# Mixers' last projections cut into pieces with their layer norm following, and the last expert's selection columns built ahead

## The reference

```python
mod = (c_act @ w_ada[l] + b_ada[l])[:, None, :]
sh1, sc1, g1, sh2, sc2, g2 = jnp.split(mod, 6, axis=-1)
h = x * (1 + sc1) + sh1
y = conformer_conv(h, ...)      # l = 0: its last step is y @ w_pw2 + b_pw2
y = fox_attention(...) @ w_o    # l = 1
x = layer_norm(ALPHA * x + (1 + g1) * y, ln_mix_g[l], ln_mix_b[l])
h = x * (1 + sc2) + sh2
y = grouped_moe(h, router_w, router_b, w_gate[l], w_up[l], w_down[l])
x = layer_norm(ALPHA * x + (1 + g2) * y, ln_ffn_g[l], ln_ffn_b[l])
```

## Time and profile before

| | us |
|---|---|
| median of 3 runs | 1313.42 (1311.5 to 1313.66) |
| profiled execution, its own time | 1311.54 |
| its span | 1309.8 |
| PE busy | 1102.8 (84%) |
| DVE busy | 444.1 (34%) |
| ACT busy | 173.9 (13%) |
| HBM read | 492.19 MB, 377 GB/s over the span |

### The profile page before, as it was taken

How to read it: one execution, slowest core, us unless ns; L and a number is a source line. 1 busy time by engine, 2 the same in 40 slices (tenths; PEclk the granted TensorE clock), 3 DMA queues, 4 the chain that set the end, 5 groups by cost and what they waited for, 6 DMA issues and landing times.

```text
span 1309.8 us, 31022 instructions
## 1 busy us (share of the span) xinstructions
PE 1102.8 (84%) x12986; PEld 627.0 (48%) x12986; DVE 444.1 (34%) x1376; ACT 173.9 (13%) x420; POOL 21.1 (2%) x61
## 2 busy tenths in 40 slices
PE   4999979769998779767899989797699996797775
PEld 1885446325554235323474854463356562453233
DVE  0698752113332113212454431521132331132124
ACT  1114131001000001001200430300001110010011
POOL 1300000000000000000000000000000000000000
PEclk9999969879999789878999989697899998898788
DMA  9985989999999999999998633899999999999992
GB/s 357 381 341 217 423 351 420 420 420 422 421 421 419 421 421 420 420 421 420 419 416 326 277 129 115 359 421 422 419 422 420 382 406 420 421 421 420 420 421 119
DMA packets 77793, 494.76 MB, mean 378 GB/s; under 512 B 7876, under 2 KB 16100, under 8 KB 20856
## 3 DMA queue, kind: packets, MB, share of 16 engines
q1 hardware_dynamic: 76752, 490.77, 91.3%
q10 hardware_dynamic: 744, 2.35, 0.5%
q0 software_dynamic: 192, 0.15, 0.0%
HBM read 492.19 MB, written 1.05 MB: 377 GB/s over the span
## 4 chain that ended last, share of the span: by engine, by line
PE 56%; DMA 35%; DVE 4%; ACT 2%; SPq 1%; issue 1%; DVEq 0%; POOLq 0%; ACTq 0%
PE PS L1122 25%; DMA ring<-in_w_up_dram 18%; PE PS L1023 6%; PE PS L1280 4%; DMA ring<-in_w_down_dram 4%; DMA ring<-in_w_gate_dram 4%; PE PS L1100 3%; PE PS L1150 2%; DMA work<-in_w_down_dram 2%; PE PS L1041 2%; DMA ring<-in_w_kvf_dram 2%; DMA work<-in_w_gate_dram 2%; PE PS L1414 2%; DMA ring<-in_w_ada_dram 2%; PE PS L921 1%; SPq L460 1%
## 5 line engine op out<-in xcount | busy, mean ns | idle before, releaser
L1122 PE MATMUL PS<-ring,work 128*32 128x256 f32 x8160 | 532.7, 412 | 121.0 <-DMA ring<-in_w_up_dram 46.5
L1122 PEld LDWEIGHTS PS<-ring,work 128*32 128x32 f32 x8160 | 272.5, 116 | 364.7 <-issue 85.7
L1762 DVE TENSOR_TENSOR work<-work,PS 128x256 f32<-128x256 f32 x43 | 18.1, 421 | 392.6 <-PE PS L1122 392.6
L1023 PE MATMUL PS<-ring,work 128*128 128x512 f32 x192 | 85.2, 604 | 0.5 <-ACT work L853 0.5
L1100 PE MATMUL PS<-hs,work 128*32 128x256 f32 x784 | 61.5, 437 | 13.7 <-DVE work L1710 13.7
L1122 PE MATMUL PS<-work 128*32 128x256 f32 x864 | 59.2, 410 | 15.4 <-DMA work<-in_w_down_dram 8.1
L700 ACT ACTIVATE work<-PS 128x256 f32<-128x256 f32 x43 | 16.5, 383 | 406.5 <-PE PS L1122 406.5
L1023 PEld LDWEIGHTS PS<-ring,work 128*128 128x128 f32 x192 | 36.9, 194 | 47.7 <-issue 46.8
L1150 PE MATMUL PS<-work 32*128 32x256 f32 x784 | 56.1, 400 | 3.8 <-DVE work L1775 3.8
L1280 PE MATMUL PS<-work,ring 128*128 128x256 f32 x256 | 57.8, 388 | 1.4 <-ACT work L632 1.4
L1874 DVE SCALAR_TENSOR_TENSOR work<-work,colv 128x256 f32<-128x256 f32 x130 | 57.8, 510 | 0.5
(11 more groups left out here) (257 smaller groups left out, 853.6 us busy)
## 6 DMA issues: line engine op xcount, KB each, us to landing
ring<-in_w_gate_dram SPq DMA_DIRECT2D x116, 1024.0 KB, 26.4
ring<-in_w_up_dram SPq DMA_DIRECT2D x116, 1024.0 KB, 26.6
ring<-in_w_down_dram SPq DMA_DIRECT2D x116, 1024.0 KB, 26.0
ring<-in_w_ada_dram SPq DMA_DIRECT2D x48, 1024.0 KB, 19.9
ring<-in_w_pw_dram SPq DMA_DIRECT2D x12, 1024.0 KB, 12.0
work<-in_w_up_dram SPq DMA_DIRECT2D x12, 1024.0 KB, 19.7
work<-in_w_gate_dram SPq DMA_DIRECT2D x12, 1024.0 KB, 26.4
work<-in_w_down_dram SPq DMA_DIRECT2D x12, 1024.0 KB, 27.7
```

Source lines behind the costliest of these rows:

```text
L1023: last = pe.matmul(PS[:, banks + 2 * t + q, :], moving[:, k, t * P:(t + 1) * P], quarter(index + h, kk, KH)[:, q * BANK:(q + 1) * BANK], s ...
L1122: last = pe.matmul(dst[SLOTS * s:SLOTS * (s + 1), :], rows[:, cc, SLOTS * q:SLOTS * (q + 1)], quarter(load + h, kk, KH)[:, QUART * s:QUART ...
```

## The change

- The load order puts `ADA1_G2` ahead of `WO`, and DVE takes it (`BY_VECTOR`).
- The last projection of either mixer runs piece by piece: `project_pieces` finishes one bank (t, q) before the next and signals `y_ready` for each. The gate row is spread after the first piece, and ACT copies it to SBUF (`g1_row`).
- DVE's `close_mixer` handles each piece (product straight from PSUM, residual, statistics), and normalises token tile 0 while the last piece is computed. The transposes are split by token tile (`turn_by_tile`) and the copies to `hT` start after both.
- In layer 0, of the four loads of `ADAKV` PE takes one before the router, one between logits and count, and two after the count; its `add_ada` stands before the signal `routed`.
- `columns` transposes all 128 rows, four times, into a whole bank, everywhere it is used.
- On DVE the columns G for the last expert's second block are built before the last but one expert's `result_of`, and each further block's inside `take_xT_late`; PE's `sum_x` in `gated` comes first, behind a wait for `GWT_copied`.

```diff
-    L_WO = L_WQ + 2
-    L_ADA1_G2 = L_WO + 2
-    L_MOE1 = L_ADA1_G2 + ADA_G
+    L_ADA1_G2 = L_WQ + 2
+    L_WO = L_ADA1_G2 + ADA_G
+    L_MOE1 = L_WO + 2
-    BY_VECTOR = (*range(L_ADA0_G2, L_ADA0_G2 + ADA_G), *range(L_ADA1_G0, L_ADA1_G0 + ADA_G))
+    BY_VECTOR = [i for first in (L_ADA0_G2, L_ADA1_G0, L_ADA1_G2) for i in range(first, first + ADA_G)]
...
+            load_wide(L_ADA1_G2, wide_ada[1][2])
             load_pair(L_WO, wo_h)
-            load_wide(L_ADA1_G2, wide_ada[1][2])
             load_experts(L_MOE1, 1)
...
+
+            def mixer_root(l, bank, first, end):
+
+                act.wait_ge(spread, (1, 4)[l])
+                act.activation(g1_row, PS[:, 4:6, :].rearrange("p b n -> p (b n)"), ACT.Copy).then_inc(spread_used, 1)
+                for t in range(TT):
+                    act.wait_ge(ln_var, norms[0] + 1)
+                    act.activation(rstd[:, t:t + 1], mv[:, t, 1:2], ACT.Sqrt, bias=eps[:, 0:1]).then_inc(ln_sd, 1)
+                    norms[0] += 1
+                    shifts[0] += 1
+                    act.wait_ge(shift_ready, shifts[0])
+                    act.activation(chunks(hs, t)[:, 1], by_chunk(xs[:, t, :])[:, 1], ACT.Identity, bias=negm[:, t:t + 1],
+                                   scale=rstd[:, t:t + 1]).then_inc(n_half, 1)
+                copy_cols(bank, first, end)
+                keep_g2(l)
+
...
-            def columns(bank, first, end):
-
-                n = end - first
+            def columns(bank):
+
                 for j in range(4):
-                    last = pe.matmul(PS[:, bank, 4 * n * j:4 * n * (j + 1)].rearrange("p (q r) -> p q r", q=4), rows[:, j:BANK:4],
-                                     ident[:, :].rearrange("p (q r) -> p q r", q=4)[:, :, first:end],
-                                     start=True, stop=True, skip_group_check=True)
+                    last = pe.transpose(PS[:, bank, P * j:P * (j + 1)], rows[:, j:BANK:4], ident[:, :])
                     if j == 0:
                         behind(last)
...
+
+            def turn_by_tile(norms, t):
+
+                pe.wait_ge(h_ready, TT * (norms - 1) + t + 1)
+                pe.wait_ge(n_half, TT * (norms - 1) + t + 1)
+                for k in range(KD):
+                    last = pe.transpose(PS[:, k // KH * 2 + t, k % KH * P:(k % KH + 1) * P], hs[:, t, k * P:(k + 1) * P],
+                                        ident[:, :])
+                    if k % KH == KH - 1:
+                        last.then_inc(h_turned, 1)
+                if t == TT - 1:
+                    hs_turned[0] += 1
...
+            def project_pieces(index, l, moving, chunk_ready=None, begun=False):
+
+                for t in range(TT):
+                    for q in range(2):
+                        for k in range(KD):
+                            h, kk = divmod(k, KH)
+                            if t == q == 0:
+                                if kk % 2 == 0:
+                                    arrived(index + h, kk // 2)
+                                if chunk_ready is not None:
+                                    pe.wait_ge(chunk_ready, k + 1)
+                            last = pe.matmul(PS[:, 2 * q + t, :], moving[:, k, t * P:(t + 1) * P],
+                                             quarter(index + h, kk, KH)[:, q * BANK:(q + 1) * BANK],
+                                             start=(k == 0 and not begun), stop=(k == KD - 1), skip_group_check=True)
+                            if k == t == q == 0:
+                                behind(last)
+                            if t == q == 1 and k == KH - 1:
+                                last.then_inc(half_free, 1)
+                        last.then_inc(y_ready, 1)
+                        if t == q == 0:
+                            pe.wait_ge(ada_added, (2, 6)[l])
+                            spread_mod(l, 2, 4)
+                owed[0] = 1
+
+            def close_mixer(index, l):
+
+                bias_rows(index, 7)
+                pe.wait_ge(acc_g2_ready, 2 * (l + 1))
+                for q in range(4):
+                    last = pe.matmul(PS[32 * q:32 * q + 32, 7, :], ones[:, 0:32], acc_g2[:, q * BANK:(q + 1) * BANK],
+                                     start=False, stop=True, tile_position=(0, 32 * q), skip_group_check=True)
+                    if q == 0:
+                        behind(last)
+                last.then_inc(ada_done, 1)
+                turn_by_tile(2 * l + 1, 0)
+                pe.wait_ge(ada_added, adas[0])
+                columns(5)
+                spread_g2(l)
+                turn_by_tile(2 * l + 1, 1)
+
...
                 if l == 0:
-                    ada_load(L_ADAKV, ADA_G - 1, 6)
+                    ada_load(L_ADAKV, 1, 6)
...
                 pe.matmul(PS[:, B_UP, E:2 * E], before[:, :], r_sel[:, 1, :], start=False, stop=True).then_inc(pos_done, 1)
+                if l == 0:
+                    for j in range(2, ADA_G):
+                        ada_load(L_ADAKV, j, 6)
...
-                def gated(last, load, before_all):
-
+                def gated(last, load, before_all, results):
+
+                    pe.wait_ge(GWT_copied, results + 1)
+                    sum_x(last + 2)
                     pe.wait_ge(XT_copied, last + (l + 1))
                     pe.wait_ge(hhT_kept, before_all + 1)
                     pe.wait_ge(sil_ready, last)
-                    sum_x(last + 2)
                     strips(load, 0, XT, gate_ps, gate_half)
+                    pe.wait_ge(yb_copied, results + 1)
                     turn_x(last + 2)
                     strips(load, 1, XT, gate_ps, gate_done)
...
-            project(L_PW2, 0, y_ready, chunk_ready=z_ready, begun=True)
-            pe.wait_ge(ada_added, 2)
...
-            last.then_inc(ada_done, 1)
-            for j in range(ADA_G - 1):
-                ada_load(L_ADAKV, j, 6)
-            pe.wait_ge(ada_added, 3)
-            spread_g2(0)
-            columns(7, 2, 4)
-            turn_n(1)
+            project_pieces(L_PW2, 0, hT, chunk_ready=z_ready, begun=True)
+            close_mixer(L_ADA0_G2, 0)
+            ada_load(L_ADAKV, 0, 6)
             moe(L_MOE0, 0)
...
-            project(L_WO, 0, y_ready, moving=QT)
-            spread_mod(1, 2, 4)
-            ada(L_ADA1_G2, 6)
-            pe.wait_ge(ada_added, 7)
-            columns(7, 5, 7)
-            turn_n(3)
-            spread_g2(1)
+            project_pieces(L_WO, 1, QT)
+            close_mixer(L_ADA1_G2, 1)
...
-                else:
-                    row = spread_banks(4)
-                    for t in range(TT):
-                        dve.wait_ge(y_read, TT * l + t + 1)
-                        last = dve.tensor_tensor(hs[:, t, :], hs[:, t, :], row, ALU.mult)
-                    last.then_inc(spread_used, 1)
-                    dve.wait_ge(spread_used, spreads[0])
-                    for t in range(TT):
...
+
+                lane_sums(index, acc_g2, acc_g2_ready, 2 * l)
+                spreads[0] += 1
+                dve.wait_ge(spread_used, spreads[0])
+
+                def piece(t, q):
+                    of = slice(q * BANK, (q + 1) * BANK)
+                    dve.wait_ge(y_ready, 4 * l + 2 * t + q + 1)
+                    link(dve.tensor_tensor(hs[:, t, of], PS[:, 2 * q + t, :], g1_row[:, of], ALU.mult))
+                    link(dve.scalar_tensor_tensor(out=xs[:, t, of], in0=xs[:, t, of], scalar=ALPHA, in1=hs[:, t, of],
+                                                  op0=ALU.mult, op1=ALU.add))
+                    return dve.bn_stats(stats[:, t, q, :], xs[:, t, of])
+
+                def variance(t):
+                    dve.bn_aggr(mv[:, t, :], stats[:, t, 0:2, :].rearrange("p q s -> p (q s)")).then_inc(ln_var, 1)
+
+                def normalise(t):
+                    dve.wait_ge(ln_sd, norms[0] + t + 1)
+                    link(dve.reciprocal(rstd[:, t:t + 1], rstd[:, t:t + 1]))
+                    dve.scalar_tensor_tensor(out=negm[:, t:t + 1], in0=mv[:, t, 0:1], scalar=-1.0, in1=rstd[:, t:t + 1],
+                                             op0=ALU.mult, op1=ALU.mult).then_inc(shift_ready, 1)
+                    dve.tensor_scalar(chunks(hs, t)[:, 0], by_chunk(xs[:, t, :])[:, 0], mv[:, t, 0:1], rstd[:, t:t + 1],
+                                      ALU.subtract, ALU.mult).then_inc(h_ready, 1)
+
+                piece(0, 0)
+                link(piece(0, 1))
+                variance(0)
+                piece(1, 0)
+                normalise(0)
+                link(piece(1, 1))
+                variance(1)
+                add_ada(*ada_next)
+                normalise(1)
+                norms[0] += 2
...
                                          op1=ALU.mult).then_inc(sel_ready, 1)
-                if l == 0:
-                    add_ada(ROW_KV, 6)
                 dve.wait_ge(totals_done, l + 1)
...
                 dve.tensor_tensor(place[1][:, :], place[1][:, :], place[0][:, :], ALU.subtract).then_inc(counted, 1)
+                if l == 0:
```

(5 more changed lines are left out.)

139 lines of the change are left out of this document (62 added, 77 removed).

## The result

The changed kernel took 1303.34 us (median of four runs, 1298.27 to 1305.46) against 1313.54 of the kernel before (four runs, 1311.5 to 1314.79): ratio 0.9922, 95% interval 0.9897 to 0.9947. Timed again it took 1300.85 (six runs, 1296.82 to 1303.28), ratio 0.991 (0.9885 to 0.9935). The forecast was 1301.1, range 1294.5 to 1309. By medians the gain is 10.2 us (11.1 the second time), against 12.3 forecast. The total held. Of its terms layer 1's close and the columns held, layer 0's and the tail's did not, and two losses were not in it; these misses cancelled, which is luck.

The account below looks back on a forecast made before the run. DMA-bound expert stretches, PE's chain from 655 us to layer 1's first freed expert tile, and the tail bound the kernel. Terms 1.0 + 1.5 + 1.0 + 7.2 + 1.6 = 12.3 us took 1313.4 to 1301.1, range 1294.5 to 1309.

Parts of the forecast that it names:

- Part 1, layer 1's close: Layer 1, projection's end to router: 9.4 us instead of 16.6, gain 7.2, bounds 6.0 to 8.0.
- "+1.1" for the row spread: Layer 1's last projection: the row spread now stands inside it and moves all later pieces by 1.1 us.
- Part 2, layer 0's hole: Layer 0's close: DMA idle of 4.9 us, set by four key/value tile slots; gain 1.5, from -1.1 to 3.4.
- PE at half clock throughout (3.64 a tile): Layer 0's close and routing: slots free at about 168, 175, 180, 188; holes together 6.0 us, a loss of 1.1.
- my full-clock case: Layer 0's tiles at 1.8 us each: first three in time, fourth at about 183.5; hole 1.5 us, gain 3.4.
- Part 3, columns: Ahead of the first projection and of the queries: four transposes replace eight matmuls, gain 1.0 us each, bounds 0 and 1.5.
- Part 4, the tail: Last expert's second block: PE no longer waits 1.64 us for DVE's columns before its gather; gain 1.6 us.
- 1.6, down to 0 if another wait takes over: Tail's gain of 1.6 us could vanish behind another wait; the up tile's second half lands at about 1276.5.
- swallow layer 1's gain: Rival: PE-bound heavy experts at 1015 to 1080 absorb layer 1's gain, leaving 5.1 us, 1308.3; 10%.
- the 17 us of that rival: Clock rival: clock stays high in closes and both routings, gain 17 us, 1296.4; 15% for 1297 or less.
- The half-clock projection: Rival: layer 1's last mixer projection never climbs from half clock, +25 us, 1326.1; 3%.
- "Pieces not closed ahead": Rival: all four pieces of the mixer close are closed at the end, 5.5 us lost, gain 6.8, 1306.6; 7%.

Follow-up runs that it names:

- columns alone: Kernel before with only the columns made by four transposes, at the three places outside the mixers' closes: 1308.73 us, ratio 0.9977 to the kernel before.
- tail alone: Kernel before with only the last expert's gather columns built earlier and its first gather put ahead of the up-projection wait: 1311.37 us, ratio 0.9995.
- dense filler: Changed kernel plus unread 512-column matmuls in layer 1's routing: with 15, 1298.56 us, ratio 0.9876; with 9, 1300.19 us, ratio 0.9911 to the kernel before.

## Why the prediction was right, and where it was not

**Part 1, layer 1's close: 7.2 forecast, 9.2 measured in the first pair of profiles** (46.19 to 37.04 from the projection's start to the router; 5.6 with the second profile of each). The other profiles say which number is the change's. The close takes 44.3 to 44.4 in the second profile of before, with the columns alone and with the tail alone, and 37.0 in the changed kernel and with the tail or the key/value tiles as before: 7.3. The part was right. The 2 us above it are luck of the first pair: the projection of before took 29.54 there, with a mean clock of 0.83, and 27.73 in those three others. The terms in detail: the chain behind the last piece was priced at 8.3 and took 8.05 (the transposes ran at the full clock, 1.06 and not 1.8; the three passes over the piece took 2.1, not 1.8; the columns were covered), and "+1.1" for the row spread is 1.26 (28.99 with it, 27.73 without, both at a granted clock of 1.00). Each of the two halves of the rewrite is shown: the matrix 5.8 us, the overlap (both layers together, and with it the clock) 17.6. The two don't add up to the gain, since each alone leaves the other's wait in the gap.

**Part 2, layer 0's hole: 1.5 forecast; start and hole together 2.5, measured 4.7.** This is the term that failed, and the step is "PE at half clock throughout (3.64 a tile)". I took the half clock of the old close for the new one, though the new one has no long gap of PE. The four tiles ran in 1.9 each, and the fourth slot was free at 178, not 188 nor even the 183.5 of my full-clock case. That case was wrong too: against the half-clock one it took off 4.5 us, where four tiles at 1.92 instead of 3.64 alone take off 6.9. Nor does the hole hang on the last us: in three of the variants one of the four tiles took 3.45 to 3.61, the gather came at 181.1 to 181.3, and the hole was 0, as in all nine profiles with pieces closed ahead. The run with pieces closed at the end gives the number for my assumption: with PE idle for 6.45 us the clock does fall, two of the four tiles take 3.6, and the hole is 9.1 us. The gain from the first to the key projection is 2.8 to 4.9 us in every pair of a profile with the old close and one with pieces closed ahead.

**Part 3, columns: 1.0 and 1.0 forecast, 0.9 and 1.5 measured**, 1.3 and 1.2 by the other pairs. Right. The Trainium skill ("TensorE: Matmul & The Clock Gate", part 4), by which transposes don't count as activity for the clock, would have made these places slower. In this trace the transposes of the close (808.35 to 812.4) ran at the full pace, with a projection's matmuls just ahead of them; the clock was down at 815 to 826, behind them, where PE was busy for 5.32 of 11 us. The old close tells more, and against the rule. In the profile of before the granted clock was 0.50 from 823.75 to 827.10 us, and PE's work there was the 16 transposes of the earlier trace rows; from 827.15 on it was 1.00. So the clock rose while PE did nothing but transposes. The other three profiles with the old close show the same in layer 1.

**Part 4, the tail: 1.6 forecast, 0.5 in the profile, 0.7 timed alone, inside the noise.** The wait went as forecast. The step that failed is "1.6, down to 0 if another wait takes over": not a wait took over but the clock, 0.86 us more for each 16 strips at 1.93 instead of 1.07.

**What I did not have in the sum:** the attention's end is 1.3 us longer, and from router to last landing 1.4 us are lost (438.1 to 439.4). The second is not shown to be the change's: the last transfer took 1.55 more in this pair (28.18 for 26.63), but 26.6 again in three of the variants of the changed kernel, and the whole stretch is 438.1 to 439.4 in the four profiles with the old close and 438.0 to 441.6 in the ten others. At the first, the clock differs. Windows of the changed kernel at the attention's end:

```profile
760.00:769.00 9.00, 6.21 (x49) 4.78 (x50) 4.57 (x23) 4.59 (x19) 0.00 (x0) 1.00 0.80 315
769.00:777.00 8.00, 5.28 (x30) 3.09 (x30) 3.18 (x9) 1.53 (x4) 0.00 (x0) 0.58 0.40 170
```

and of the second profile of the kernel before:

```profile
760.00:769.00 9.00, 9.00 (x59) 7.40 (x58) 5.10 (x26) 4.36 (x18) 0.00 (x0) 1.00 0.06 10
769.00:777.00 8.00, 5.20 (x41) 3.84 (x41) 3.19 (x15) 3.10 (x13) 0.00 (x0) 0.89 0.95 390
777.00:785.00 8.00, 4.79 (x32) 2.61 (x31) 2.21 (x7) 1.91 (x5) 0.00 (x0) 0.90 0.30 125
```

Over the last 9.5 us ahead of the mixer projection, the same sparse work in both, the granted clock is 0.64 in the changed kernel (0.50 in its second profile) and 0.83 and 0.82 in the two of before (1.00 with the columns or the tail alone). Over all profiles this stretch of the attention takes 63.5 to 64.8 us in the four with the old order, and 65.5 to 67.2 in eight of the ten others; the two exceptions, 64.2 (matrix back on PE and loaded late again) and 64.8 (key/value tiles as before), have a clock of 0.84 and 0.82 there. So the loss goes with the clock; why the clock falls sooner in the new kernel is open.

The sum of the terms as measured is 0.9 + 3.8 + 1.5 - 1.3 + 9.2 - 1.4 + 0.5 = 13.2, against my 12.3, for the first pair of profiles. The total was right because misses cancelled: +2.3 in layer 0 and +2.0 in layer 1 (the clock of one profile) stand against -1.1 in the tail and -2.7 of losses not seen, with +0.4 in the columns.

**The rivals.** The expert stretch did not swallow layer 1's gain: the landing of the last gate tile came 12.7 us sooner (10.1 in the second pair), and the DMA share at 1015 to 1080 was 0.96 in both. What dense filler won at the entry did not reach the end: from router to last landing it is 438.4 and 440.6 us with it, 439.4 and 441.4 without. The clock stayed high through both closes of the first profile, but not in the routing of layer 1 (0.60 over the 11 us behind the router), so the 17 us of that rival did not come. The half-clock projection did not come about (7.13 and 20.87 for 16 and 48 instructions, 0.43 each in the second). "Pieces not closed ahead" was priced at 5.5 us lost; made in a run of its own it cost 17.6: 8.6 in layer 1's close (6.5 of wait, and 2.1 since I had left out that the clock falls while PE waits for DVE), and 10.2 ahead of the key projection, since I had priced layer 1 alone.

## To carry to other kernels

A pass over rows that follows a matmul piece by piece pays for its own length and again for the clock of what follows, because PE does not stand idle: price both, and read the clock of the new stretch from a stretch with the new one's gaps, not the old one's. A serial matrix in the gap must leave with it, or most of the gap stays. A wait removed where PE's clock changes between executions and variants, as behind a single landing, showed its length here only in the two profiles that were at the upper level; it needs timed runs, and more of them than its size first suggests.
